# Another order for the minima and low parts of the neighbourhood attention, and stick-breaking weights stored column by column

## The chip, the core and the metric

The kernel runs on one core of one Trainium2 chip. The metric is the device time of one execution in microseconds (us); three runs of the kernel before gave 1026.44 to 1029.01, median 1027.77. One further execution was recorded by the profiler, and every row below comes from it.

The engines by the names of the profile: PE is TensorE (matmuls), PEld its weight loads, DVE VectorE, ACT ScalarE, POOL GpSimd, SP the queue that issues most loads.

## What is computed

The kernel is a chain of two networks in fp32 over 256 tokens of width 1024: two layers (a pooling mixer, then stick-breaking attention, each followed by a gated feed-forward), then a third layer with neighbourhood attention and a long convolution side by side, a gated merge and a feed-forward. The change touches two places.

Stick-breaking attention (16 heads of 64, 272 tokens, the first 16 of them meta tokens that are keys for all):

```python
z = jnp.einsum('bqhd,bkhd->bhqk', q, k) * (HEAD_DIM ** -0.5)
mask = kpos[None, :] < qpos[:, None]
log_keep = jnp.where(mask, jax.nn.log_sigmoid(-z), 0.0)
later = lax.cumsum(log_keep, axis=3, reverse=True) - log_keep
a = jnp.where(mask, jnp.exp(jax.nn.log_sigmoid(z) + later), 0.0)
return jnp.einsum('bhqk,bkhd->bqhd', a, v)
```

Neighbourhood attention (8 heads of 64; 256 keys of the grid, rotated, with a bias, and 256 context keys):

```python
s_nb = jnp.einsum('brqhd,brikhd->bhrqik', grid(q_rot), k_band) * scale + bias[None]
s_nb = jnp.where(col_ok[:, None, :], s_nb, NEG_INF)
s_ctx = jnp.einsum('brqhd,bchd->bhrqc', grid(q), k_ctx) * scale
p = jax.nn.softmax(jnp.concatenate([s_nb, s_ctx], axis=-1), axis=-1)
o = p_nb @ v_band + p_ctx @ v_ctx
```

Beside it a short convolution over 12 column blocks of 128 (`hy`), whose first eight results are turned for a long convolution.

## The kernel before

**Products.** Each fp32 operand is split into a high part (fp32r, ScalarE's copy) and a low part (the difference, VectorE), and a product is three matmuls: high x high, low x high, high x low. Weights arrive as `raw` (three buffers of 1 MB, loaded by SP as soon as the low parts made from the old contents exist), are cast by ScalarE into `wh` and lowered by VectorE into `wl`. Such a piece of 128x1024 is a "half"; six halves are held, and a half may be written once the half six places earlier is spent. `casts` (line 430) and `rests` (line 447) issue every cast or low part that has become possible up to a given point; `rests` can be limited by `most`.

**The order.** Each engine runs a written queue in order; waits are on semaphores that count named moments. So the order of the calls in `sb_pe`, `sb_act`, `sb_dve` (stick-breaking) and `second_pe`, `second_act`, `second_dve`, `second_pool` (neighbourhood) is the order of the work.

**Stick-breaking, lines 1291 to 1716.** The loop runs over p = 0 to 7, pairs of heads (h = 0, 1), and in each over two query tiles (qt = 0: 152 keys, qt = 1: 272 keys). Per pair TensorE makes the scores (`scores_pe`), the projections of q and k for pair p+2 and of v for pair p+1, turns v (`vt_pe`) and the weights (`turns_pe`), and sums the output of pair p-1 (`out_pe`). Keys 32 to 151 and 152 to 271 are turned in two pieces of 120. The first 32 keys are the tail: both heads' tails lie above each other in 64 rows, so that `out_pe` handles both in one group of three matmuls. Before, head 0's tail is turned by a transpose into rows 0 to 31, and head 1's into rows 32 to 63 by `turn` (line 1312), an ordinary fp32 product with the identity matrix; the row shows it as a MATMUL of line 93, a transpose as one of line 96. ScalarE makes |z|, exp, ln (`softs`), the final exponential `weights` into `as_[2h+qt]`, and the high parts `ath`, `tth`; VectorE makes the maximum (`soft`), the scan (`later`), the difference (`kept`) and the low parts `atl`, `ttl`, `vl`; `kvf` scales a projection out of PSUM.

**Neighbourhood, lines 1917 to 2336.** The loop runs over p = 0 to 3, each with two heads (h) and two query tiles (qt), kk = 4p + 2h + qt. Per step kk: `na_scores` on TensorE (12 or 6 matmuls into bank 3 or 4), `least` on VectorE (adds the bias of buffer kk % 3, takes the minimum of the negative), `soft` on ScalarE (exponential with its sum), `shares` on VectorE (reciprocal, scaling), `na_turn` (four transposes), `ath`/`atl` for the high and low parts, `na_av`, then `oh`/`ol`. The queries are rotated: `perm_pe`, `turn1`, `turn2`, then high and low parts `quh`, `qul`, `qrh`, `qrl` into `QQ`, whose other head's 64 rows must be zero. POOL adds the bias and the mask (`b`, kk) into BB. The convolution blocks are `hy_pe`, `conv` on both engines, `hy_turn` and `turned`.

Of the kernel before, what the change touches and what calls it, by code (L numbers as in the profile page):

```python
# [238 lines left out]
class Kernel:  # L239
# [252 lines left out]
    def memory_sb(self):  # L492
# [17 lines left out]
        self.as_ = [at(f"a{i}", T1) for i in range(4)]  # L510
# [822 lines left out]
    def turns_pe(self, P, p, h, qt):  # L1333
        S, a = self.S, self.as_[2 * h + qt]
        if qt == 0:
            self.claim(P, 5 + h, (S["sb_v"], ("atl", p, h)))
        if h + qt == 0:
            self.claim(P, 7, (S["sb_v"], ("ol", p)))
        tb, o_bank = self.ps[5 + h], self.ps[7]
        P.wait_ge(S["sb_a"], ("at", p, h, qt))  # L1340
        if qt == 0:
            P.tr(tb[0:120, 256:384], a[:, 32:152], self.ident)
            self.turn(P, o_bank, h, slice(0, 128), a[:, 0:32]).then_inc(S["sb_p"], ("t", p, h, 0))
        else:
# [4 lines left out]
    def out_pe(self, P, p):
# [101 lines left out]
    def sb_act(self, A):  # L1451
# [1628 lines left out]
```

## Time and profile before

| | |
|---|---|
| timed runs | 1026.44, 1027.77, 1029.01 us, median 1027.77 |
| profiled execution | 1023.1 us, its span 1020.8 us |
| TensorE / its weight loads | 984.4 us (96%) / 952.7 us (93%) of the span |
| VectorE | 823.2 us (81%) |
| ScalarE | 565.0 us (55%) |
| GpSimd | 110.7 us (11%) |
| HBM traffic | 192.17 MB, 188 GB/s on average |

Busy time is an average over stages. Stick-breaking runs from about 255 to 387 us of the span and the neighbourhood stage from about 621 to 712 us; each has to be read by itself. A matmul's end is modelled in these rows, so that TensorE shows itself busy for some tenths of a microsecond in which nothing new is issued; the start of the next weight load is the better mark. TensorE's granted clock is full throughout both stages.

### The profile page before, as it was taken

How to read it: one execution, taken by the hardware profiler on the slowest of the kernel's cores; microseconds unless marked ns; L12 is line 12 of the kernel's file. 1: busy time of each engine (PE TensorE's matmuls, PEld its weight loads, DVE VectorE, ACT ScalarE, POOL GpSimd, SP SyncE). 2: the span in 40 equal slices, each digit the busy share in tenths (PEclk: the TensorE clock that was granted, in tenths of full speed). 3: DMA queues.
4: the chain of work that ended last, by engine and by line, in shares of the span. 5: the costliest groups of instructions: out<-in, count | busy, mean ns of one | idle time of the engine just before them, and what ended most of it. 6: DMA issues, size and time to landing. Idle time of an engine off the chain costs nothing.

```text
span 1020.8 us, 19465 instructions
## 1 busy us (share of the span) xinstructions
PE 984.4 (96%) x7932; PEld 952.7 (93%) x7932; DVE 823.2 (81%) x1386; ACT 565.0 (55%) x1062; POOL 110.7 (11%) x128
## 2 busy tenths in 40 slices
PE   7999999999999999999999999899999999999996
PEld 6899999999888889999999998888999989999996
DVE  7989898887889867999979868888998668776543
ACT  6745454445766646555554535665554466665432
POOL 4100000111000004002203310221001100000000
PEclk9999999999999999999999999999999999999999
DMA  9554657665433314888867813333335436555441
GB/s 283 229 194 184 239 204 243 238 238 195 147 134 101 128 62 172 341 317 301 288 222 287 312 39 148 139 107 113 134 138 210 162 124 218 212 190 175 159 164 41
DMA packets 33880, 192.17 MB, mean 188 GB/s; under 512 B 4976, under 2 KB 6272, under 8 KB 15104
## 3 DMA queue, kind: packets, MB, share of 16 engines
q1 hardware_dynamic: 23440, 157.36, 42.7%
q10 hardware_dynamic: 6912, 25.17, 7.3%
q0 software_dynamic: 3440, 8.42, 2.7%
q8 instruction: 62, 1.02, 0.4%
q14 instruction: 26, 0.21, 0.1%
HBM read 187.78 MB, written 3.15 MB: 187 GB/s over the span
## 4 chain that ended last, share of the span: by engine, by line
PE 70%; DVE 19%; ACT 6%; issue 3%; DMA 1%; POOL 0%; DVEq 0%; ACTq 0%; POOLq 0%
PE ps L93 69%; DVE wl L70 6%; ACT wh L67 2%; DVE a L70 1%; DVE b L70 1%; DVE natl L70 1%; PE ps L96 1%; DMA raw<-w 1%; ACT s L67 1%; DVE s L84 1%; DMA fz<-fz 1%; DVE s L77 1%; DVE x L73 0%; DVE tmp L73 0%; DVE x L70 0%
## 5 line engine op out<-in xcount | busy, mean ns | idle before, releaser
L70 DVE TENSOR_TENSOR wl<-raw,wh 128x1024 fp32r<-128x1024 f32 x283 | 342.6, 1225 | 22.7 <-ACT wh L67 22.3
L67 ACT ACTIVATE wh<-raw 128x1024 fp32r<-128x1024 f32 x286 | 296.2, 1049 | 25.1 <-PE ps L93 10.2
L93 PE MATMUL ps<-xh,wh 128*128 128x256 f32 (+1 forms) x992 | 278.4, 281 | 4.2 <-DVE wl L70 2.7
L93 PE MATMUL ps<-xh,wl 128*128 128x256 f32 (+1 forms) x992 | 276.8, 279 | 0.0
L93 PE MATMUL ps<-xl,wh 128*128 128x256 f32 x992 | 275.7, 278 | 0.0
L93 PE MATMUL ps<-xt,wh 128*128 128x272 f32 (+1 forms) x1120 | 218.3, 290 | 2.2 <-DVE fg L70 1.0
L93 PEld LDWEIGHTS ps<-xh,wh 128*128 128x128 f32 x992 | 186.7, 188 | 5.5 <-issue 2.4
L93 PEld LDWEIGHTS ps<-xl,wh 128*128 128x128 f32 x992 | 187.1, 189 | 0.0
L93 PEld LDWEIGHTS ps<-xh,wl 128*128 128x128 f32 x992 | 186.7, 188 | 0.2
L93 PEld LDWEIGHTS ps<-xt,wh 128*128 128x128 f32 x1120 | 177.4, 188 | 5.4 <-issue 2.0
L93 PE MATMUL ps<-xt,wl 128*128 128x272 f32 (+1 forms) x560 | 160.1, 286 | 0.0
L93 PE MATMUL ps<-hl,wh 128*128 128x256 f32 (+1 forms) x528 | 149.7, 283 | 0.0
L93 PE MATMUL ps<-hh,wh 128*128 128x256 f32 (+1 forms) x528 | 149.6, 283 | 0.0
L93 PE MATMUL ps<-hh,wl 128*128 128x256 f32 (+1 forms) x528 | 149.6, 283 | 0.0
L93 PEld LDWEIGHTS ps<-xt,wl 128*128 128x128 f32 x560 | 105.7, 189 | 0.3
L93 PEld LDWEIGHTS ps<-hl,wh 128*128 128x128 f32 x528 | 100.5, 190 | 0.0
L93 PEld LDWEIGHTS ps<-hh,wh 128*128 128x128 f32 x528 | 99.4, 188 | 0.1
L93 PEld LDWEIGHTS ps<-hh,wl 128*128 128x128 f32 x528 | 99.1, 188 | 0.0
L67 ACT ACTIVATE hh<-fh 128x256 fp32r<-128x256 f32 (+1 forms) x66 | 27.9, 422 | 102.9 <-DVE fh L70 79.1
L70 POOL TENSOR_TENSOR acc<-acc,sq 128x256 f32<-128x256 f32 (+1 forms) x30 | 33.7, 1124 | 443.0 <-ACT sq L67 443.0
L67 ACT ACTIVATE sq<-x 128x256 f32<-128x256 f32 (+1 forms) x43 | 17.6, 420 | 96.7 <-DVE x L70 51.4
L84 DVE CUSTOM_DVE_ANT_0 ada<-ada,cb 128x1024 f32<-128x1024 f32 x42 | 57.2, 1361 | 0.1
(350 smaller groups left out, 1596.8 us busy)
## 6 DMA issues: line engine op xcount, KB each, us to landing
raw<-w SPq DMA_DIRECT2D x141, 1024.0 KB, 4.9
ada<-ada ACTq DMA_DIRECT2D x42, 512.0 KB, 4.5
cb<-ada ACTq DMA_DIRECT2D x6, 512.0 KB, 4.2
raw<-w SPq DMA_DIRECT2D x4, 512.0 KB, 6.5
spare<-w SPq DMA_DIRECT2D x2, 1024.0 KB, 9.6
spectra<-ev POOLq DMA_DIRECT2D x8, 256.0 KB, 4.9
skew<-rpb POOLq DMA_DIRECT2D x8, 192.0 KB, 3.6
x<-x POOLq DMA_DIRECT2D x2, 544.0 KB, 9.1
```

Source lines behind the costliest of these rows:

```text
L67: return Issued(self.e and self.e.activation(out, src, func, **kw))
L70: return Issued(self.e and self.e.tensor_tensor(out, a, b, op))
L77: return Issued(self.e and self.e.tensor_scalar(out, src, s1, s2, op0=op0))
L84: return Issued(self.e and self.e.tensor_tensor_reduce(out, a, b, scale, start, op0, op1, accum))
L93: return Issued(self.e and self.e.matmul(out, stat, mov, start=start, stop=stop))
L96: return Issued(self.e and self.e.transpose(out, src, ident))
```

## The change

In stick-breaking attention the four weight tiles `as_` become one tile `aw`, in which the two heads of one query tile lie column by column (head 0 in the even columns, head 1 in the odd ones). The first 64 columns hold the first 32 keys of both heads, so that one transpose of 64 columns turns both tails; it is issued with head 1's turns, and the tail's rows are now interleaved. The same is done for v: `vf` is written without its first 32 keys, which go into a 64-column tile `vtail` in two steps of 64 rows with stride-two writes (the other head's columns are zero), and one transpose turns it. The copies and low parts of the v tail become one 64x128 step each. `turn` is gone.

In the neighbourhood stage the eight zero fills of `QQ` go from VectorE (64 rows each) to GpSimd (128 rows each), where they stand ahead of the bias sums; for p < 3, `least(4p+3)` and `shares(4p+3)` go from the start of the next pair to the end of their own, around `atl`; the DFT table's split (FH, FL) goes from before the loop to behind `conv(0)`; some low parts of the first pair are issued later; and TensorE makes the first two scores of p = 0 before `hy_pe(2)`, as for the others.

The diff, cut to its core:

```diff
-        self.as_ = [at(f"a{i}", T1) for i in range(4)]
+        self.aw = at("a", 4 * T1)
+        self.vtail = [area(f"vt{i}", 64) for i in range(2)]
...
-        P.tr(b[0:32, 256:384], f[:, 0:32], self.ident)
-        self.turn(P, b, 1, slice(256, 384), f[:, 0:32]).then_inc(S["sb_p"], ("vt", p))
-
-    def turn(self, P, bank, h, c, a):
-        if h == 0:
-            return P.tr(bank[0:32, c], a, self.ident)
-        return P.mm(bank[32:64, c], a, self.ident, True, True)
+        P.tr(b[0:64, 256:384], self.vtail[p % 2][:, :], self.ident).then_inc(S["sb_p"], ("vt", p))
+
+    def weight(self, h, qt):
+
+        return self.aw[:, 2 * T1 * qt + h:2 * T1 * (qt + 1):2]
...
+        S, a = self.S, self.weight(h, qt)
         if qt == 0:
             self.claim(P, 5 + h, (S["sb_v"], ("atl", p, h)))
-        if h + qt == 0:
+        if h and qt == 0:
             self.claim(P, 7, (S["sb_v"], ("ol", p)))
         tb, o_bank = self.ps[5 + h], self.ps[7]
         P.wait_ge(S["sb_a"], ("at", p, h, qt))
         if qt == 0:
-            P.tr(tb[0:120, 256:384], a[:, 32:152], self.ident)
-            self.turn(P, o_bank, h, slice(0, 128), a[:, 0:32]).then_inc(S["sb_p"], ("t", p, h, 0))
+            o = P.tr(tb[0:120, 256:384], a[:, 32:152], self.ident)
         else:
             P.tr(tb[0:120, 384:512], a[:, 32:152], self.ident)
-            P.tr(tb[0:120, 128:256], a[:, 152:272], self.ident)
-            self.turn(P, o_bank, h, slice(128, 256), a[:, 0:32]).then_inc(S["sb_p"], ("t", p, h, 1))
+            o = P.tr(tb[0:120, 128:256], a[:, 152:272], self.ident)
+        if h:
+            o = P.tr(o_bank[0:64, 128 * qt:128 * (qt + 1)], self.aw[:, 2 * T1 * qt:2 * T1 * qt + 64], self.ident)
+        o.then_inc(S["sb_p"], ("t", p, h, qt))
...
-            for k in (0, 1):
-                s = slice(32 * k, 32 * k + 32)
-                A.act(th[s, 64 * k:64 * k + 64], b[s, 256 + 64 * k:320 + 64 * k], ACT.Copy).then_inc(
-                    S["sb_a"], ("wth", p, k))
+            A.act(th[:, :], b[0:64, 256:384], ACT.Copy).then_inc(S["sb_a"], ("wth", p))
...
-            A.act(self.as_[i][:, :w], self.cs[(4 * p + i) % 3][:, :w], ACT.Exp).then_inc(S["sb_a"], ("at", p, h, qt))
+            A.act(self.weight(h, qt)[:, :w], self.cs[(4 * p + i) % 3][:, :w], ACT.Exp).then_inc(S["sb_a"], ("at", p, h, qt))
...
+        def vf(p):
+
+            f, ft, b = self.vf[p % 2], self.vtail[p % 2], self.ps[self.bank[("v", p)]]
+            if p > 1:
+                V.wait_ge(S["sb_p"], ("vt", p - 2))
+            V.wait_ge(S["sb_g"], ("zero",))
+            V.wait_ge(S["proj"], ("v", p))
+            V.tt(f[:, 32:], b[:, 32:T1], R[:, 32:], ALU.mult).then_inc(S["sb_v"], ("vmain", p))
+            for k in (0, 1):
+                s = slice(64 * k, 64 * k + 64)
+                o = V.tt(ft[s, k:64:2], b[s, 0:32], R[s, 0:32], ALU.mult)
+            o.then_inc(S["sb_v"], ("vf", p))
...
-            for k in (0, 1):
-                s, c = slice(32 * k, 32 * k + 32), slice(64 * k, 64 * k + 64)
-                V.tt(tl[s, c], b[s, 256 + 64 * k:320 + 64 * k], th[s, c].bitcast(F32), ALU.subtract).then_inc(
-                    S["sb_v"], ("wtl", p, k))
+            V.tt(tl[:, :], b[0:64, 256:384], th[:, :].bitcast(F32), ALU.subtract).then_inc(S["sb_v"], ("wtl", p))
...
-            if p:
-                self.na_scores(P, p, 0, 0), self.na_scores(P, p, 0, 1)
+            self.na_scores(P, p, 0, 0), self.na_scores(P, p, 0, 1)
             self.hy_pe(P, 3 * p + 2)
-            if p == 0:
-                self.na_scores(P, p, 0, 0), self.na_scores(P, p, 0, 1)
...
-        A.wait_ge(S["ld_dftf"], ("load",))
-        A.act(self.FH[:, :], self.dftf[:, :], ACT.Copy).then_inc(S["hy_a"], ("tab", 0))
         for p in range(4):
             qf(p), quh(p, 0), quh(p, 1)
             self.casts(A, W.spent(("nq", p)))
...
                     turned(3 * p - 1)
                 ath(2 * p - 1, 0), ath(2 * p - 1, 1)
             conv(3 * p)
+            if p == 0:
+                A.wait_ge(S["ld_dftf"], ("load",))
+                A.act(self.FH[:, :], self.dftf[:, :], ACT.Copy).then_inc(S["hy_a"], ("tab", 0))
...
-        V.wait_ge(S["na_p"], ("v", 3))
-        for i, s in enumerate(self.QQ):
-            for t in s:
-                r0 = 64 * (1 - i)
-                o = V.memset(t[r0:r0 + 64, :].bitcast(F32), 0.0)
-        o.then_inc(S["na_v"], ("zero",))
         vl(2), vl(3), vl(0), vl(1)
-        self.rests(V, first + 8)
-        V.wait_ge(S["hy_a"], ("tab", 0))
-        V.tt(self.FL[:, :], self.dftf[:, :], self.FH[:, :].bitcast(F32), ALU.subtract).then_inc(S["hy_v"], ("tab", 0))
+        self.rests(V, first + 8, most=3)
         for p in range(4):
-            if p:
-                least(4 * p - 1), shares(4 * p - 1)
             qul(p, 0), qul(p, 1)
             turn1("q", p)
             if p:
                 ol(2 * p - 2)
-            self.rests(V, W.spent(("nq", p)))
+            if p > 1:
+                self.rests(V, W.spent(("nq", p)))
             if p:
                 atl(2 * p - 1, 0), atl(2 * p - 1, 1)
             conv(3 * p)
-            turn2("q", p), qrl(p, 0), qrl(p, 1)
-            self.rests(V, W.spent(("hy", 3 * p)))
+            if p == 0:
+                V.wait_ge(S["hy_a"], ("tab", 0))
+                V.tt(self.FL[:, :], self.dftf[:, :], self.FH[:, :].bitcast(F32), ALU.subtract).then_inc(
+                    S["hy_v"], ("tab", 0))
+            turn2("q", p)
+            if p == 0:
+                qrl(p, 0), qrl(p, 1)
+                self.rests(V, W.spent(("nq", 0)))
+            else:
+                qrl(p, 0), qrl(p, 1)
+                self.rests(V, W.spent(("hy", 3 * p)))
             if p:
                 ol(2 * p - 1)
             conv(3 * p + 1)
-            self.rests(V, W.spent(("hy", 3 * p + 1)))
+            if p:
+                self.rests(V, W.spent(("hy", 3 * p + 1)))
             least(4 * p), least(4 * p + 1), shares(4 * p), shares(4 * p + 1)
+            if p == 0:
+                self.rests(V, W.spent(("hy", 0)))
             conv(3 * p + 2)
             least(4 * p + 2)
-            self.rests(V, W.spent(("hy", 3 * p + 2)))
+            if p:
+                self.rests(V, W.spent(("hy", 3 * p + 2)))
+            if p < 3:
+                least(4 * p + 3)
             atl(2 * p, 0), atl(2 * p, 1), shares(4 * p + 2)
+            if p < 3:
+                shares(4 * p + 3)
+            if p == 0:
+                self.rests(V, W.spent(("hy", 2)))
...
+        G.wait_ge(S["na_p"], ("v", 3))
+        for s in self.QQ:
+            for t in s:
+                o = G.memset(t[:, :].bitcast(F32), 0.0)
+        o.then_inc(S["na_g"], ("zero q",))
```

## Rows read from the trace of the kernel before

**Rows 1.** The page, section 4: the chain that ended last, shares by engine.
```profile
PE 70%; DVE 19%; ACT 6%; issue 3%; DMA 1%; POOL 0%; DVEq 0%; ACTq 0%; POOLq 0%
```

**Rows 2.** Busy us (instructions) of PE, PEld, DVE, ACT, POOL; clock, DMA, GB/s.
```profile
282.50:298.35 15.85, 15.85 (x121) 14.05 (x120) 14.03 (x31) 10.81 (x29) 0.00 (x0) 1.00 0.20 67
...
650.31:672.11 21.80, 20.27 (x168) 19.39 (x168) 18.95 (x39) 13.86 (x30) 4.99 (x6) 1.00 0.32 115
```

**Rows 3.** PEld in stick-breaking, timeline: start, us, operation, count [idle <-releaser].
```profile
279.25 0.54 PEld L96 LDWEIGHTS ps<-cst,a 128*120 128x120 f32 x5
...
270.90 0.27 PEld L96 LDWEIGHTS ps<-cst,vf 128*120 128x120 f32 x3
...
271.37 0.14 PEld L93 LDWEIGHTS ps<-cst,vf 128*32 128x32 f32 x2 [0.21 <-issue]
...
271.71 0.19 PEld L93 LDWEIGHTS ps<-kh,qh 128*128 128x128 f32 x1 [0.20 <-issue]
...
281.94 0.14 PEld L96 LDWEIGHTS ps<-cst,a 128*120 128x120 f32 x1 [0.21 <-ACT a L67]
...
282.53 0.19 PEld L93 LDWEIGHTS ps<-xt,wh 128*128 128x128 f32 x1 [0.20 <-issue]
```

**Rows 4.** PEld by form, 624 to 716: count | busy, mean ns | idle.
```profile
L96 PEld LDWEIGHTS ps<-cst,s 128*128 128x128 f32 x64 | 7.0, 140 | 8.1 <-DVE s L77 7.8
...
L96 PEld LDWEIGHTS ps<-cst,tmp 128*128 128x128 f32 x16 | 2.5, 206 | 1.8 <-DVE tmp L73 1.8
```

**Rows 5.** Timelines of ACT and DVE in one stick-breaking pair.
```profile
286.39 0.49 ACT L67 ACTIVATE ath<-ps 120x384 fp32r<-120x384 f32 x1 [2.03 <-PE ps L93]
...
286.92 0.56 DVE L70 TENSOR_TENSOR atl<-ps,ath 120x384 fp32r<-120x384 f32 x1 [0.56 <-ACT ath L67]
...
289.51 0.76 DVE L73 SCALAR_TENSOR_TENSOR l<-ps,l 128x152 f32<-128x152 f32 x2 [0.58 <-ACT l L67]
...
297.40 0.33 ACT L67 ACTIVATE a<-c 128x152 f32<-128x152 f32 x1 [0.68 <-DVE c L70]
```

**Rows 6.** Groups by form, DVE, whole run: a small step out of PSUM.
```profile
L70 DVE TENSOR_TENSOR wtl<-ps,wth 32x64 fp32r<-32x64 f32 x16 | 3.3, 209 | 0.3
```

**Rows 7.** Timelines of DVE and PE, neighbourhood pair p = 1 and its end.
```profile
661.69 0.68 DVE L84 CUSTOM_DVE_ANT_0 s<-ps,bias 128x512 f32<-128x512 f32 x1
...
668.02 1.29 DVE L70 TENSOR_TENSOR natl<-ps,nath 128x512 fp32r<-128x512 f32 x2 [0.23 <-ACT nath L67]
...
671.39 0.16 DVE L87 RECIPROCAL small<-small 128x1 f32<-128x1 f32 x1 [0.88 <-ACT s L67]
...
672.13 0.66 PE L96 MATMUL ps<-cst,s 128*128 128x128 f32 x4 [1.01 <-DVE s L77]
```

**Rows 8.** Timelines of DVE, ACT and PE, first neighbourhood pair.
```profile
621.50 0.27 DVE L90 MEMSET nqh<- 64x256 f32 x1 [3.13 <-PE ps L93]
...
624.16 0.60 ACT L67 ACTIVATE vvh<-ps 128x512 fp32r<-128x512 f32 x1 [0.78 <-PE ps L93]
...
634.60 0.50 PE L96 MATMUL ps<-cst,tmp 128*128 128x128 f32 x2 [1.61 <-DVE tmp L73]
...
639.91 0.69 DVE L84 CUSTOM_DVE_ANT_0 s<-ps,bias 128x512 f32<-128x512 f32 x1
```

**Rows 9.** Timelines of POOL and DVE: zero fills of BB, bias sums, low part.
```profile
598.52 0.83 POOL L90 MEMSET bias<- 128x256 f32 x3
...
599.30 1.44 POOL L70 TENSOR_TENSOR bias<-skew,cmask 128x256 f32<-128x256 f32 x2
...
644.94 1.66 POOL L70 TENSOR_TENSOR bias<-skew,cmask 128x256 f32<-128x256 f32 x1 [1.89 <-DVE small L84]
...
644.77 1.23 DVE L70 TENSOR_TENSOR wl<-raw,wh 128x1024 fp32r<-128x1024 f32 x1
```

**Rows 10.** Timeline of PE behind the stage; the page's section 6, weight loads.
```profile
738.03 0.38 PE L93 MATMUL ps<-yh,gh 128*128 128x256 f32 x1 [0.57 <-DVE yl L70]
...
raw<-w SPq DMA_DIRECT2D x141, 1024.0 KB, 4.9
```

More of the change, by code:

```diff
@@ L1304, in vt_pe @@
         S, f = self.S, self.vf[p % 2]
-        b = self.next_bank(P, ("vt", p), (S["sb_v"], ("wtl", p, 1)))
+        b = self.next_bank(P, ("vt", p), (S["sb_v"], ("wtl", p)))
         P.wait_ge(S["sb_v"], ("vf", p))
@@ L1353, in out_pe @@
         P.wait_ge(S["sb_v"], ("vl", p))
-        P.wait_ge(S["sb_v"], ("wtl", p, 1))
+        P.wait_ge(S["sb_v"], ("wtl", p))
         P.wait_ge(S["sb_v"], ("ttl", p))
@@ L1444, in sb_pool @@
                 G.memset(self.pad(t, 1).bitcast(F32), 0.0)
-            for t in (th, tl):
-                o = G.memset(t[:, :].bitcast(F32), 0.0)
+        for t in self.vtail:
+            o = G.memset(t[:, :], 0.0)
         o.then_inc(S["sb_g"], ("zero",))
@@ L1510, in weights @@
             if p:
-                A.wait_ge(S["sb_p"], ("t", p - 1, h, qt))
+                A.wait_ge(S["sb_p"], ("t", p - 1, 1, qt))
             else:
@@ L1603, in ql, with kf @@
             V.tt(l[s, c], self.qf[p % 2][s, :], h[s, c].bitcast(F32), ALU.subtract).then_inc(S["sb_v"], ("ql", p, k))
-        def kvf(k, p):
-            f = (self.kf if k == "k" else self.vf)[p % 2]
+        def kf(p):
             if p > 1:
-                V.wait_ge(*((S["sb_v"], ("kl", p - 2)) if k == "k" else (S["sb_p"], ("vt", p - 2))))
+                V.wait_ge(S["sb_v"], ("kl", p - 2))
             V.wait_ge(S["norm_v"], ("r", "m1"))
-            V.wait_ge(S["proj"], (k, p))
-            V.tt(f[:, :], self.ps[self.bank[(k, p)]][:, :T1], R[:, :], ALU.mult).then_inc(S["sb_v"], (k + "f", p))
+            V.wait_ge(S["proj"], ("k", p))
+            V.tt(self.kf[p % 2][:, :], self.ps[self.bank[("k", p)]][:, :T1], R[:, :], ALU.mult).then_inc(
+                S["sb_v"], ("kf", p))
+        def vf(p):
[9 more added lines that the diff above has]
+            o.then_inc(S["sb_v"], ("vf", p))
         def kl(p):
@@ L1621, in vl @@
             b = self.ps[self.bank[("vt", p)]]
[L1622 removed]
+            V.wait_ge(S["sb_a"], ("wth", p))
             V.tt(self.pad(l), b[0:120, 0:256].rearrange("p (t k c) -> p t k c", t=2, k=2), self.pad(h).bitcast(F32),
                  ALU.subtract).then_inc(S["sb_v"], ("vl", p))
[L1625 to L1628 removed]
+            V.tt(tl[:, :], b[0:64, 256:384], th[:, :].bitcast(F32), ALU.subtract).then_inc(S["sb_v"], ("wtl", p))
         def part(p, h, qt):
@@ L1670, in sb_dve @@
         for p in (0, 1):
-            qf(p), kvf("k", p), ql(p, 0), ql(p, 1), kl(p)
+            qf(p), kf(p), ql(p, 0), ql(p, 1), kl(p)
             self.rests(V, W.spent(("k", p)))
-        kvf("v", 0)
+        vf(0)
         for p in range(8):
@@ L1695, in sb_dve @@
                 ql(p + 2, 1)
-                kvf("k", p + 2)
+                kf(p + 2)
                 self.rests(V, W.spent(("k", p + 2)), True)
@@ L1701, in sb_dve @@
             if p < 7:
-                kvf("v", p + 1)
+                vf(p + 1)
             atl(p, 1)
@@ L1939, in na_scores @@
         P.wait_ge(S["na_v"], ("krl", p))
-        P.wait_ge(S["na_v"], ("zero",))
+        P.wait_ge(S["na_g"], ("zero q",))
         P.wait_ge(S["na_v"], ("qul", p, h))
@@ L2067, in quh @@
                 A.wait_ge(S["na_p"], ("s", 4 * p - 3 + 2 * h))
-            A.wait_ge(S["na_v"], ("zero",))
+            A.wait_ge(S["na_g"], ("zero q",))
             A.wait_ge(S["na_a"], ("qf", p))
@@ L2252, in least @@
                 V.wait_ge(S["na_p"], ("t", kk - 3))
-            V.wait_ge(S["na_v"], ("zero",))
+            V.wait_ge(S["na_g"], ("zero q",))
             V.wait_ge(S["na_g"], ("b", kk))
```

2 lines of the change are left out of this document (removed).

## The prediction

> **What bounds the kernel now.** I read the chain that ended last first, then the busy time by stretch, then each engine's timeline in the two stages that the diff touches. Over the whole run TensorE carries 70% of the chain [rows 1], so the question is whether the two stages are among the exceptions. They differ. In the stick-breaking stage (255 to 387 us) one pair of heads takes 15.85 us, TensorE has no idle time in it and VectorE is busy 14.03 us; in the neighbourhood stage (621 to 712 us) one pair takes 21.80 us, VectorE is busy 18.95 us, and its weight-load column shows TensorE free for some 2.4 us of it [rows 2]. So stick-breaking is set by TensorE with the softmax loop close behind, and the neighbourhood stage by VectorE's queue with the waits inside it.
>
> **Stick-breaking, TensorE.** Three transposes hold the weight load for 0.27 us, five for 0.54 [rows 3]; I take 0.09 us each and 0.1 for the way back to ordinary work. Head 1's part of the 32-key tail is no transpose but a true fp32 product against the identity: two passes with an idle weight load of 0.20 us before and after. The block of vt_pe (three transposes and one such product) takes 0.81 us; with three transposes alone 3 x 0.09 + 0.1 = 0.37, so 0.44 is saved. The block of turns_pe(1,0) takes 0.59; two transposes take 0.28, so 0.31 is saved [rows 3]. turns_pe(1,1) has one transpose more and should save between the two, 0.39. Head 0's block loses two of its five transposes: 0.18. Sum 1.32 us per pair. The six long transposes now load every second column. The nearest rows: a stride-two load of tmp is busy 0.206 us, a packed one 0.140 [rows 4]; six times 0.066 would be 0.4. Packed loads are issued well under 0.140 apart (three in 0.27), so most of such a time overlaps, and I take 0.1. TensorE's own time per pair falls by 1.2 to 14.65 us.
>
> **Stick-breaking, the loop behind it.** That much is not to be had, since turns_pe(1,0) already waits 0.21 us for ScalarE's weights [rows 3]. The loop: turns_pe(1,0) at 281.94, the value projection, turns_pe(1,1), ScalarE's ath at 286.39, then tth, a cast, abs, exp, ln, VectorE's first maximum at 289.51 (after 0.58 idle), VectorE without a gap to the difference that feeds the exponential at 297.40, and turns_pe(1,0) again, 15.85 after its last start [rows 5]. What it loses: 0.31 in turns_pe(1,0); about 0.23 in turns_pe(1,1) up to its last result (the way back isn't on this path), less 0.02 for strides; and on VectorE one of two tail subtractions. Those are 32x64 at 0.21 us each [rows 6]; one 64x128 in their place I take at 0.3, 0.18 less with the gap between them. Sum 0.52 + 0.18 = 0.70. The new vf makes one product into three: the long one is 32 columns shorter, and each small one has 64x32 elements, half the row length of the 32x64 ones (0.21 [rows 6]), so up to 0.4 more. It stands ahead of atl(1) and ttl on VectorE's queue, where VectorE now waits 0.56 us for ath [rows 5]; that wait hides it, and without the wait it would cost 0.4 per pair. ScalarE's second tail copy (0.21) goes too, off the loop. ScalarE's exponentials now write every second word. No row of the kernel before shows such a write on ScalarE; from the packed 0.33 us I take no change, and as the far end a doubling, +0.33 on the loop. VectorE's queue time is 15.85 - 1.54 of named idle = 14.3, plus 0.2 net, 14.5: it isn't the bound. So the pair goes to 15.15 us: 0.7 x 5 = 3.5 us for the five steady pairs (turns_pe(1,0) from 266.08 to 345.36).
>
> The ends: pair 0 gains 0.2 (the tail copy stands ahead of its exponentials; vf's extra 0.4 is taken up by a later wait of VectorE for ScalarE). From 345.36 to the end of pair 6 the projections and the output matmuls fill TensorE, and its savings count in full: 0.31 + 0.39 + 0.44 + 0.18 + 0.31 + 0.23 = 1.86, less 0.1 for strides; pair 7's chain runs over ScalarE's tail copies, another 0.15. After turns_pe(7,1,0), which waits for ScalarE, 0.31 + 0.39 remain. Stage: 0.2 + 3.5 + 1.9 + 0.7 = **6.3 us**. The feed-forward layer behind it fills TensorE, so the gain is kept.
>
> **Neighbourhood, steady pairs.** VectorE idles in five places: 0.27, 0.23 (atl waits for ath), 0.88 (shares(4p+3) waits for its exponential, right behind least(4p+3)), 0.46 (ol) and 0.48 (qrl) (two of them in [rows 7]). With least(4p+3) ahead of atl and shares(4p+3) behind shares(4p+2), the exponential runs beside atl: ath has 0.65 us more, the 0.23 and the 0.88 go, and ol comes behind an output matmul that is no longer stalled, for 0.4 more. TensorE's wait of 1.01 us for shares(4p+3) [rows 7] goes with it. least(4p+3) needs scores(1,1), done 1.2 us before VectorE reaches it; if they were late, atl, shares(4p+2) and TensorE's na_av would queue behind it. The pair goes from 21.80 to about 20.4; TensorE's floor is 21.8 - 2.1 of stalls = 19.7. Two pairs (p = 1 and 2) give 2.8 us; pair 3 keeps its order.
>
> **Neighbourhood, the first pair.** Eight zero fills leave VectorE (0.27 each, behind 3.13 us of waiting for the v projection [rows 8]). But vl's last step waits for ScalarE's copy of the last v bank at 624.16, so only 0.66 us is gained there. Walking on with the same durations: vl ends at 625.45, three low parts at 629.2, qul to 630.3, conv(0) at 631.35 (0.6 idle, for ScalarE), the table's low part, the turn, qrl to 635.05, two low parts, conv(1), least(0) at 638.25 against 639.91 [rows 8]. TensorE loses its 1.61 us wait at hy_turn [rows 8] and finds about 1.5 us at the scores moved ahead of hy_pe(2), since qrl(0,0) is ready at 634.65. Then the deferred low parts come due: six between least(0) and least(4) where there were four, 2 x 1.14 = 2.3 us, less 1.1 of waits saved, so that least(4) comes at 661.3 against 661.69 [rows 7]. The first pair yields **0.4 us**. The loads behind deferred halves stay ahead: SP's load behind half 181 is issued at 642.8, lands some 4.9 us later [rows 10] and is cast after 651. The POOL fills: 128x256 took 0.28 us each [rows 9], eight 2.2 us from 621.4, done at 623.7, where ScalarE first needs them at 629.4. On POOL's queue the bias sums stand behind them; three at 0.75 are ready at 626, needed at 638. Stage: 0.4 + 2.8 = **3.2 us**, kept, since VectorE also sets the pace of the following stage (TensorE waits for it at 738 [rows 10]) and nothing there is tied to an outer event.
>
> The bias sums now run at 624 to 626 us, beside vl and VectorE's first low part. In the trace a low part that had started 0.2 us before a bias sum took 1.23 us, as any other, and the bias sum 1.66 instead of 0.72 [rows 9]: POOL, the later one, gave way. The Trainium skill (SBUF — State Buffer, section "SBUF: two separate sides") has it that a VectorE operation with two SBUF inputs and a GpSimd operation that reads SBUF exclude each other for a whole instruction, and that whoever starts first wins; by that rule the first low part may be held back by the rest of the third bias sum, up to 0.72 us, and the stage would give 2.5 us instead of 3.2. The row agrees with the rule for the case where VectorE is first; no row shows POOL first.
>
> **The sum.** 6.3 + 3.2 = 9.5 us. The profiled execution took 1023.1 us around a span of 1020.8; it becomes 1013.6. It lies 4.7 us under the median of the timed runs, 1027.77, with the same kernel; against the median the sum gives **1018.3 us** (0.991).
>
> **Rivals.** (a) The loop doesn't bind and TensorE's full 1.2 us per pair comes off: 0.5 x 5 more, 1015.8. Against it: the 0.21 us wait that stands there already. 12%. (b) VectorE binds: vf's small steps cost like whole ones (0.4 each), or the exponentials double; then 0.3 to 0.4 of the 0.7 goes, the stage gives 4, the time is 1020.5. For it: VectorE at 14.5 of 15.15. 18%. (c) The neighbourhood order only moves the waits: the first pair's new stalls grow, or low parts are held back by POOL, and 0.5 to 1 us is left: 1020.8. For it: my own walk, where 1.66 us gained at least(0) shrank to 0.4. 12%. (d) Both (b) and (c), and less: within 3 us of before. 7%. (e) Slower: ScalarE's stride-two writes. Its exponentials take 1.52 us of 10.8 busy per pair; if a strided write took k times as long, ScalarE would bind from k = 4.5 on; at k = 6 the pair is 18.2 us, seven pairs cost 16.5, and the time is 1027.8 + 16.5 - 3.2 = 1041. Against it: TensorE's strided load is busy only half as long again. 3%, and 1% for the sum of small things. (f) The forecast, 1016.3 to 1020.3: 47%.
>
> **How the numbers follow.** (a) to (c) and (f) are 89% and faster by more than 0.3%, about the least that a measurement of this kernel can tell from no change; (d) is no change, (e) slower: 0.89, 0.07, 0.04. The range takes in (a) with the profiled run's offset, so down to 1012.5, and (b) and (c) to 1023.
>
> **What would show it.** Right: turns_pe(1,0) starts 15.1 to 15.2 us apart with a wait of 0.4 to 0.7 us for ScalarE; no fp32 product in the turns; 0.88 gone from shares(4p+3), pairs 20.4 us apart, least(0) 1.7 us earlier but least(4) only 0.4 us (each after taking off the first stage's shift). Wrong: a pair of 15.6 (VectorE or ScalarE binds) or 14.7 (no loop); a low part behind a bias sum at 626; a long ScalarE exponential.

## The result and the profile after

Four runs of the changed kernel took 1009.55 to 1012.26 us, median **1011.57 us**; with a fourth run beside it the kernel before has the median 1027.11. The ratio is 0.9859, 95% interval 0.9838 to 0.9880: faster, and by more than the forecast's 9.5 us (0.991). A second set of runs, on other occasions (r1 below), gave 1010.38 against 1020.13 us, 0.9897 [0.9875, 0.9919]; one run of the kernel before in that set took 1202.17 us at a granted clock of 0.753, and the ratio leaves it out. The changed kernel repeats; the kernel before was 7 us slower in the first set. So the gain is between 9.8 and 15.5 us, and the traces must say what of it is the change.

The profiled executions: span 1007.5 us against 1020.8, 13.3 less. Where one and the same operation stands in both traces, after less before:

| point | shift, us |
|---|---|
| TensorE, first scores of stick-breaking | +0.18 |
| first addition of the stage's output to x (382.84 before) | -7.03 |
| end of the second feed-forward layer | -7.91 |
| first rotation of k, ahead of the neighbourhood stage | -8.94 |
| least(12) | -12.25 |
| TensorE, first product with gh (738.03 before) | -12.24 |
| third feed-forward layer, middle / end | -10.94 / -13.25 |

Stick-breaking gave 7.21 us (forecast 6.3), the neighbourhood stage 3.31 (forecast 3.2). The other 2.74 came where the diff changes nothing.

Busy time by stretch of the changed kernel, columns as in [rows 2], one pair of each stage:

```profile
280.97:295.92 14.95, 14.53 (x114) 13.74 (x115) 14.05 (x32) 10.42 (x29) 0.00 (x0) 1.00 0.23 82
652.30:672.87 20.57, 19.22 (x161) 18.42 (x160) 18.80 (x41) 14.02 (x29) 5.01 (x6) 1.00 0.35 120
```

The pairs are 14.95 and 20.57 us long where they were 15.85 and 21.80. VectorE's busy time in the stick-breaking pair did not fall (14.05 us where it was 14.03): the stage is fuller, not emptier.

The weight loads of that stick-breaking pair (to be held against [rows 3]):

```profile
280.97 0.22 PEld L96 LDWEIGHTS ps<-cst,a 128*120 128x120 f32 x2 [0.49 <-DVE c L70]
...
284.19 0.34 PEld L96 LDWEIGHTS ps<-cst,a 128*120 128x120 f32 x3
...
285.34 0.19 PEld L96 LDWEIGHTS ps<-cst,vf 128*120 128x120 f32 x2 [0.25 <-DVE vt L70]
285.50 0.11 PEld L96 LDWEIGHTS ps<-cst,vt 128*64 128x64 f32 x1
...
295.92 0.22 PEld L96 LDWEIGHTS ps<-cst,a 128*120 128x120 f32 x2 [0.50 <-DVE c L70]
```

No load of line 93 is left among them: the true fp32 products and their 0.20 us on either side are gone. Two things are new. turns_pe(1,0) waits 0.50 us, which the forecast had said (0.4 to 0.7). And vt_pe waits 0.25 us for vf's small products, which it had not. The releaser named in the first and last row is VectorE's c, but c is only what ScalarE's exponential reads; what turns_pe(1,0) needs is that exponential's result `a`, which ends at 295.80 (295.46 and 0.34 long, below), just ahead of the load at 295.92.

ScalarE and VectorE in the same pair (to be held against [rows 5] and [rows 6]):

```profile
284.84 0.49 ACT L67 ACTIVATE ath<-ps 120x384 fp32r<-120x384 f32 x1 [1.50 <-PE ps L96]
286.43 0.56 ACT L67 ACTIVATE u<-ps 128x152 f32<-128x152 f32 x2
...
291.17 0.38 ACT L67 ACTIVATE oh<-ps 128x256 fp32r<-128x256 f32 x1 [0.58 <-PE ps L93]
...
295.46 0.34 ACT L67 ACTIVATE a<-c 128x152 f32<-128x152 f32 x1 [0.69 <-DVE c L70]
```

```profile
284.90 0.38 DVE L70 TENSOR_TENSOR vt<-ps,r 64x32 f32<-64x32 f32 x2
285.36 0.56 DVE L70 TENSOR_TENSOR atl<-ps,ath 120x384 fp32r<-120x384 f32 x1
...
287.79 0.76 DVE L73 SCALAR_TENSOR_TENSOR l<-ps,l 128x152 f32<-128x152 f32 x2 [0.42 <-ACT l L67]
...
290.35 0.27 DVE L70 TENSOR_TENSOR wtl<-ps,wth 64x128 fp32r<-64x128 f32 x1
290.55 0.40 DVE L73 SCALAR_TENSOR_TENSOR qf<-ps,r 128x256 f32<-128x256 f32 x1
...
294.05 0.32 DVE L73 SCALAR_TENSOR_TENSOR l<-ps,l 128x152 f32<-128x152 f32 x1 [0.15 <-ACT l L67]
```

And the one step of the kernel before that the forecast had passed over, ScalarE's abs of head 0:

```profile
287.99 0.73 ACT L67 ACTIVATE u<-ps 128x152 f32<-128x152 f32 x2
```

The exponential writes every second word in 0.34 us (0.33 before). atl(1) follows vf without a wait where it waited 0.56. The two abs take 0.56 where they took 0.73. The one tail subtraction, 0.27 us long, frees VectorE 0.20 us after its start (290.35 to 290.55).

The neighbourhood stage, first VectorE, then GpSimd, then TensorE (to be held against [rows 7] and [rows 8]):

```profile
616.79 1.90 DVE L70 TENSOR_TENSOR wl<-raw,wh 128x1024 fp32r<-128x1024 f32 x1 [0.25 <-ACT wh L67]
618.62 1.21 DVE L70 TENSOR_TENSOR wl<-raw,wh 128x1024 fp32r<-128x1024 f32 x1
...
622.39 1.00 DVE L73 SCALAR_TENSOR_TENSOR tmp<-ps,cst,tmp 128x255 f32<-128x255 f32 x2 [0.18 <-ACT tmp L67]
...
629.36 0.68 DVE L84 CUSTOM_DVE_ANT_0 s<-ps,bias 128x512 f32<-128x512 f32 x1
...
638.61 0.15 DVE L87 RECIPROCAL small<-small 128x1 f32<-128x1 f32 x1
...
652.30 0.68 DVE L84 CUSTOM_DVE_ANT_0 s<-ps,bias 128x512 f32<-128x512 f32 x1
...
672.87 0.68 DVE L84 CUSTOM_DVE_ANT_0 s<-ps,bias 128x512 f32<-128x512 f32 x1
```

```profile
614.27 0.31 POOL L90 MEMSET nqrl<- 128x256 f32 x1
...
616.86 0.75 POOL L70 TENSOR_TENSOR bias<-skew,cmask 128x256 f32<-128x256 f32 x1
```

```profile
625.84 0.36 PE L93 MATMUL ps<-kkh,nqrh 128*128 128x256 f32 x1 [1.69 <-DVE nqrl L70]
```

The wait of 0.88 us ahead of shares(4p+3) is gone (638.61 has none). TensorE waits 1.69 us at the moved scores (forecast 1.5). A low part of 1.90 us, where the next takes 1.21, stands beside the third bias sum (616.86).

### The profile page after: what moved, and what is told of

It reads as the page before. It is cut to its first block, busy times and chain, and to the rows that moved or that the text cites. A ratio compares the mean times of both kernels' runs of the same rounds, so it can differ in the third digit from the quotient of the medians.

```text
span 1007.5 us, 19368 instructions
## 1 busy us (share of the span) xinstructions
PE 970.8 (96%) x7884; PEld 947.9 (94%) x7884; DVE 821.9 (82%) x1386; ACT 563.0 (56%) x1054; POOL 111.5 (11%) x134
## 4 chain that ended last, share of the span: by engine, by line
PE 67%; DVE 19%; ACT 8%; issue 3%; DMA 2%; POOL 0%; SPq 0%; DVEq 0%; ACTq 0%
PE ps L93 66%; DVE wl L70 6%; ACT wh L67 3%; DMA raw<-w 2%; PE ps L96 1%; DVE a L70 1%; DVE b L70 1%; ACT u L67 1%; DMA cst<-cst 1%; DVE s L77 1%; DVE c L81 1%; DVE l L73 1%; ACT s L67 1%; DVE natl L70 0%; ACT a L67 0%
```

## The experiments

All were profiled; a ratio is against the kernel before, run on the same occasion. The kernels e3, e4, k3, n1, n2, n3 and s1 have one timed run each, the profiled one, so they are read by their traces alone. Read from each trace: the stick-breaking stage (first scores to first addition to x), its pair (mean of the five from pair 0 to pair 5), then from the first rotation of k to least(0) and to least(4), the pairs p = 1 and 2, and a tile of the third feed-forward layer's second half.

| kernel | stage | pair | least(0) | least(4) | p = 1, 2 | tile |
|---|---|---|---|---|---|---|
| before | 127.08 | 15.86 | 36.31 | 58.09 | 21.80, 21.80 | 7.77 |
| after | 119.87 | 14.93 | 34.70 | 57.64 | 20.57, 20.17 | 7.48 |
| e1_sb_only | 119.93 | 14.93 | 36.30 | 58.09 | 21.79, 21.79 | 7.77 |
| e2_na_only | 127.15 | 15.86 | 34.72 | 57.66 | 20.47, 20.28 | 7.77 |
| e3_turns_only | 121.96 | 15.18 | 36.30 | 58.09 | 21.80, 21.79 | 7.77 |
| e4_tail_only | 123.43 | 15.33 | 36.33 | 58.12 | 21.79, 21.79 | 7.77 |
| s1_tail_twice | 121.33 | 15.11 | 34.72 | 57.65 | 20.49, 20.27 | 7.77 |
| k1_vt_later | 118.52 | 14.69 | 34.71 | 57.64 | 20.47, 20.18 | 7.77 |
| k3_vt_later_cast_later | 118.55 | 14.69 | 34.70 | 57.64 | 20.46, 20.27 | 7.48 |
| k4_all_three | 117.44 | 14.47 | 34.70 | 57.63 | 20.46, 20.29 | 7.48 |
| n1_least_late | 119.93 | 14.92 | 34.71 | 62.52 | 21.78, 21.78 | 7.77 |
| n2_fills_vector | 119.95 | 14.92 | 34.70 | 57.63 | 20.46, 20.19 | 7.48 |
| n3_scores_late | 119.80 | 14.91 | 34.70 | 57.63 | 20.46, 20.18 | 7.48 |
| r1_changed_again | 119.82 | 14.92 | 34.71 | 57.65 | 20.56, 20.18 | 7.48 |

**The two parts apart.** e1 has the diff's hunks up to `sb_dve`, e2 those from `na_scores` on.

> The whole stick-breaking part of the change alone, the neighbourhood stage as before. Between the two traces (before, changed) the stick-breaking stage gave 7.2 us and the neighbourhood stage 3.3; the other 2.8 us of 13.3 came in stages that the diff doesn't touch (the second and third feed-forward layers). If the parts are independent: turns_pe(1,0) 14.95 us apart, the stage ends 7.2 us earlier, the neighbourhood pairs keep their 21.80, and the whole is 7 to 10 us faster (0.990 to 0.993). If the gain outside the stages hangs on the change as a whole (another place of the instructions or tiles) it is anything between 5 and 10 us; if it hangs on the stick-breaking part, near 10.

> The neighbourhood part alone (fills to GpSimd, low parts deferred, scores and minima moved), stick-breaking as before. Mine: pairs 20.6 and 20.2 us apart where they were 21.80, the stage gives 3.3 us, 0.9968 of the time before. Rival: part of the 3.3 us came from a better phase after the shorter stick-breaking stage (loads in time), then 2 us or less. With what the untouched stages vary by, the whole lies between 2 and 6 us faster.

e1: 0.9921 [0.9900, 0.9942]; e2: 0.9972 [0.9953, 0.9990]. The product is 0.9893, the forecast's 0.991 and r1's 0.9897 within its error. Each stage moves as it does in the whole, to 0.1 us (table), so the parts are independent. Both have the slow tile of 7.77 us.

**Stick-breaking in halves.** In both, the 32-key rows of weights and of v are in different orders (one side interleaved, the other not), so the tails' product is not the reference's; the instructions are the same.

e3 has `weights` and `turns_pe` as changed, and vf, vt_pe, wth and wtl as before:

```diff
+        self.aw = at("a", 4 * T1)
...
         self.turn(P, b, 1, slice(256, 384), f[:, 0:32]).then_inc(S["sb_p"], ("vt", p))
```

e4 the other way round:

```diff
         self.as_ = [at(f"a{i}", T1) for i in range(4)]
+        self.vtail = [area(f"vt{i}", 64) for i in range(2)]
...
+        P.tr(b[0:64, 256:384], self.vtail[p % 2][:, :], self.ident).then_inc(S["sb_p"], ("vt", p))
```

> Of the stick-breaking part only the interleaved weights and the joint transposes in turns_pe; vf, vt_pe and the tail of v as before, the neighbourhood as before. By my forecast's steps the loop loses 0.31 in turns_pe(1,0) and 0.21 in turns_pe(1,1): pair 15.33 us. By the rival reading of the changed trace (a term of the loop was missed in the tail part, because vt_pe stands between the two scores of head 0 that ScalarE waits for) the same 15.3 here, and the missing 0.2 us is in e4. If instead the turns save more on the path than I reckoned: 15.1. Slower than 15.85 if strided writes of ScalarE cost.

> Of the stick-breaking part only the 32-key tail of v: vf in three products, one joint transpose in vt_pe, one copy and one subtraction; the weights and turns_pe as before. By my forecast's steps only one tail subtraction is on the loop: 15.85 - 0.18 = 15.67 us a pair, and the 0.44 us saved in vt_pe is off it. By the rival reading vt_pe's saving brings scores(0,1) forward, for which ScalarE's second abs waits, and this part alone gives 0.35 to 0.45: 15.4 to 15.5 us. If VectorE bound, vf's 0.4 would show and the pair be 15.8 or more.

Measured 0.67 and 0.53 us less a pair, together 1.20, where the whole gives 0.93. Expected were 0.52 and, by the forecast, 0.18; the rival reading had 0.35 to 0.45 for e4, so both parts gave more than either account. Three rows of each, ScalarE's abs, VectorE's step behind the tail subtractions and head 1's first maximum; e3, with turns_pe(1,0) at 281.57:

```profile
287.01 0.59 ACT L67 ACTIVATE u<-ps 128x152 f32<-128x152 f32 x2
...
291.44 0.42 DVE L73 SCALAR_TENSOR_TENSOR qf<-ps,r 128x256 f32<-128x256 f32 x1
...
294.89 0.32 DVE L73 SCALAR_TENSOR_TENSOR l<-ps,l 128x152 f32<-128x152 f32 x1
```

and e4, with turns_pe(1,0) at 281.06:

```profile
287.11 0.56 ACT L67 ACTIVATE u<-ps 128x152 f32<-128x152 f32 x2
...
291.23 0.41 DVE L73 SCALAR_TENSOR_TENSOR qf<-ps,r 128x256 f32<-128x256 f32 x1
...
294.60 0.32 DVE L73 SCALAR_TENSOR_TENSOR l<-ps,l 128x152 f32<-128x152 f32 x1
```

The second abs needs scores(p,0,1), and vt_pe stands ahead of those on TensorE. Before, the two abs took 0.73 us, in e3 0.59 and in e4 0.56: either half brings the scores forward, so 0.14 to 0.17 us belongs to both and is counted twice in their sum. That is the term that the forecast missed when it left the saving in vt_pe, and turns_pe(1,1)'s way back to ordinary work, out of the loop. Most of the rest of the difference stands at head 1's first maximum: it starts 3.45 us behind the step after the tail in e3 and 3.37 in e4 (3.44 before), but 3.50 in the changed kernel, where it waits for ScalarE. (e3's one run took 1016.44 us, e4's 1018.43.)

**How much slack VectorE has.**

```diff
                 s = slice(64 * k, 64 * k + 64)
+                V.tt(self.vmore[s, k:64:2], b[s, 0:32], R[s, 0:32], ALU.mult)
                 o = V.tt(ft[s, k:64:2], b[s, 0:32], R[s, 0:32], ALU.mult)
```

> The changed kernel, with vf's two small products (64x32, 0.19 us each) made twice, the second time into a tile that nobody reads: 0.38 us more of VectorE per pair in front of atl(1) and ttl. My theory, that the loop through TensorE and ScalarE binds and VectorE has slack (it waits 0.42 us for the first ln of the next pair): pair 14.95 to 15.05 us. Rival, VectorE's queue is what binds at 14.95 and where the gain above my 15.15 ended: pair 15.3 us.

15.11: neither. Both numbers had priced the added products at 0.38 us, and they took 0.20. From the first small product to atl(1) it is 0.62 us instead of 0.46, and the last small product ends 0.59 us behind the first's start instead of 0.38:

```profile
285.49 0.17 DVE L70 TENSOR_TENSOR vm<-ps,r 64x32 f32<-64x32 f32 x1
...
286.11 0.56 DVE L70 TENSOR_TENSOR atl<-ps,ath 120x384 fp32r<-120x384 f32 x1
```

TensorE's wait at vt_pe grew by the same 0.20, and ScalarE's wait ahead of oh with it:

```profile
286.13 0.19 PEld L96 LDWEIGHTS ps<-cst,vf 128*120 128x120 f32 x2 [0.45 <-DVE vt L70]
...
291.94 0.39 ACT L67 ACTIVATE oh<-ps 128x256 fp32r<-128x256 f32 x1 [0.76 <-PE ps L93]
```

From 0.25 to 0.45 us, and the pair from 14.93 to 15.11: what the products took reached the pair nearly whole. That number alone would suit a loop over VectorE's queue as well. The waits speak against that one: VectorE's for head 0's ln fell from 0.42 to 0.26, but its wait for ScalarE ahead of head 1's first maximum rose from 0.15 to 0.34. So at 14.93 the path seems to lead from vf's products through TensorE (vt_pe, the q projection, out_pe) to oh, a cast and head 1's abs; k1 below settles it.

**The loop that binds after.** Three variants of the changed kernel. All have the first of these edits, k3 and k4 the second (for p > 0), k4 alone the third (for p < 6):

```diff
-            if 0 < p < 7:
-                self.vt_pe(P, p)
             self.scores_pe(P, p, 0, 1)
+            if 0 < p < 7:
+                self.vt_pe(P, p)
...
-                self.casts(A, W.spent(("q", p + 2)))
                 softs(p, 1)
+                self.casts(A, W.spent(("q", p + 2)))
...
-                self.kv_pe(P, "v", p + 1)
+                self.kv_pe(P, "v", p + 1, 0, 3)
             self.turns_pe(P, p, 1, 1)
+                self.kv_pe(P, "v", p + 1, 3)
```

> The changed kernel with vt_pe behind scores(p,0,1) instead of between head 0's two scores. My theory of the 14.95 us: two loops lie within 0.15 us of each other, one through VectorE's queue behind ath(1), one through TensorE (turns_pe(1,0), the v projection, scores(0,0), a wait of 0.25 us for vf's small products ahead of vt_pe, q projection, out_pe) to ScalarE's oh, a cast and head 1's abs. The wait goes, so TensorE's loop loses 0.25 and the pair falls by no more than VectorE's queue lets it, 0.1 us: 14.85. Rival: TensorE's loop alone binds, pair 14.70. Other rival: TensorE isn't on it, pair 14.95.

> As k1_vt_later, and ScalarE's cast of the weights' half that stands between its q copy and head 1's abs (0.95 us) comes behind head 1's ln. The loop over oh gets up to 0.4 us of slack more, until head 1's scores are what abs waits for. If VectorE's queue binds after k1, nothing changes: 14.85; if the loop over oh binds, 14.5. Slower (15.2 or more) if the later cast holds up VectorE's low part or TensorE's products of that half.

> As k3_vt_later_cast_later, and the v projection is cut behind its third tile, with turns_pe(1,1) in the gap. ath(1) needs turns_pe(1,1), which in the changed kernel waits behind the whole projection though its weights are ready 1.8 us earlier (ScalarE is idle 1.50 us ahead of ath). This takes the projection out of the loop over ath: its start comes 1.5 us earlier, head 0's abs then waits for its scores, VectorE's first maximum comes 0.4 us earlier, and the pair goes to 14.4 to 14.6 us, near TensorE's own 14.2 to 14.3. Rival: TensorE's extra break costs as much as it gives (0.1 per break), or VectorE's vf, now ahead of a ready atl(1), becomes the bound: 14.8 or more.

k1: 14.69, 0.24 us less and so practically the whole wait of 0.25; my 14.85 was too careful about VectorE's queue. ScalarE's oh now waits 0.23 us for TensorE, and VectorE has no wait left ahead of head 1's maxima. k3: nothing, 14.69 (one run, 1007.76 us), so after k1 the loop over oh isn't what binds. k4: 14.47, as expected; ath(1) starts 2.15 us behind turns_pe(1,0) (282.75 against 280.60), where it started 3.87 behind (284.84 against 280.97). Rows of k1, then of k4:

```profile
291.22 0.38 ACT L67 ACTIVATE oh<-ps 128x256 fp32r<-128x256 f32 x1 [0.23 <-PE ps L93]
...
296.08 0.22 PEld L96 LDWEIGHTS ps<-cst,a 128*120 128x120 f32 x2 [0.61 <-DVE c L70]
```

```profile
282.75 0.48 ACT L67 ACTIVATE ath<-ps 120x384 fp32r<-120x384 f32 x1
...
295.05 0.22 PEld L96 LDWEIGHTS ps<-cst,a 128*120 128x120 f32 x2 [0.21 <-issue]
```

k4's stick-breaking stage is 2.4 us shorter than the changed kernel's, which no other stage gives back. Its time was 1008.51 us against 1021.69, 0.9865 [0.9845, 0.9886], k1's 1009.42, 0.9866 [0.9842, 0.9890]. That beats the kernel before; that it beats the changed one is shown in the stage alone, since the two were not timed beside each other and the ratios overlap.

**The neighbourhood change, piece by piece undone.**

n1 takes back the move of least(4p+3), n2 that of the fills, n3 that of the first pair's scores:

```diff
         for p in range(4):
+            if p:
+                least(4 * p - 1), shares(4 * p - 1)
...
-            if p < 3:
-                least(4 * p + 3)
             atl(2 * p, 0), atl(2 * p, 1), shares(4 * p + 2)
-            if p < 3:
-                shares(4 * p + 3)
```

```diff
-                o = G.memset(t[:, :].bitcast(F32), 0.0)
...
+                o = V.memset(t[r0:r0 + 64, :].bitcast(F32), 0.0)
```

```diff
+            if p:
+                self.na_scores(P, p, 0, 0), self.na_scores(P, p, 0, 1)
             self.hy_pe(P, 3 * p + 2)
+            if p == 0:
+                self.na_scores(P, p, 0, 0), self.na_scores(P, p, 0, 1)
```

> The changed kernel, but least(4p+3) and shares(4p+3) again stand at the head of the next pair, as before; the rest of the neighbourhood change stays. Mine: the waits of 0.23 (atl) and 0.88 (shares) come back and the pairs go from 20.57 and 20.17 back to 21.6 or more; least(0) stays where it is (629.36 less what the stages ahead differ by), and least(4) comes 0 to 0.5 us later. Rival: the deferred low parts and the scores bring the pairs down, and this move alone gives less than half: pairs of 21.0 or less.

The pairs are back at 21.78, so the move of least(4p+3) is worth all 1.2 and 1.6 us of them. But least(4) came 4.9 us later, where 0 to 0.5 was expected. VectorE, TensorE and again VectorE of n1:

```profile
643.37 0.68 DVE L84 CUSTOM_DVE_ANT_0 s<-ps,bias 128x512 f32<-128x512 f32 x1
...
651.58 0.48 DVE L73 SCALAR_TENSOR_TENSOR tmp<-ps,cst,tmp 128x255 f32<-128x255 f32 x1 [2.10 <-ACT tmp L67]
```

```profile
645.68 0.66 PE L96 MATMUL ps<-cst,s 128*128 128x128 f32 x4 [3.56 <-DVE s L77]
```

With the low parts deferred, two of them stand ahead of a late least(3); shares(3) comes at 645.14, TensorE waits 3.56 us for it with hy_pe's next products behind, and the convolution at 651.58 waits 2.10 us for what follows from those. Part of that is TensorE's clock. Busy 0.94 of the 4.5 us from 642.0 to 646.5, it then had a granted clock of 0.5 (1.2 GHz) for 3.41 us from 647.04, just when those products ran; columns of the first row as in [rows 2]:

```profile
647.00:650.40 3.40, 3.40 (x19) 3.40 (x18) 1.71 (x3) 1.64 (x5) 0.00 (x0) 0.51 0.20 84
```

```profile
648.04 0.41 PE L93 MATMUL ps<-xh,wl 128*128 128x256 f32 x1
648.26 0.41 PE L93 MATMUL ps<-xl,wh 128*128 128x256 f32 x1
```

Sixteen products started 0.213 us apart where 0.117 is usual, an estimated 1.5 us of the 4.9. Up to least(4) n1 takes 4.4 us more than the kernel before, in one execution: some 3 of them by the waits and the rest, by that estimate, by the clock. The rest of the new order is a loss in that pair unless least(4p+3) moves too. Whether the clock falls in every execution of n1 isn't shown. (n1's one run: 1021.98 us, n2's 1011.41, n3's 1009.56, s1's 1013.93, the kernel before beside them 1022.83.)

> The changed kernel with the eight zero fills back on VectorE behind the last v projection. By my forecast they were worth 0.66 us of least(0)'s 1.66 us (the fills take 2.2 us, but vl's last step waits for ScalarE in any case), so least(0) comes 0.6 to 0.7 us later than in the changed kernel (and the three deferred low parts give the rest), least(4) and the pairs after it 0.2 to 0.7 later, not more. Rival: the fills were worth 1.3 us or more.

> The changed kernel with the first pair's scores of head 0 again behind hy_pe(2). TensorE's wait of 1.69 us for the moved scores goes; the products of hy_pe(2), 2.8 us, stand ahead of the scores instead. Mine: VectorE reaches least(0) 3.5 us after the low part of the rotated q, so the scores in the new place come at about 629.9 instead of 627.2 and least(0) waits for them some 0.5 to 1 us, least(4) 0 to 0.5 later; no gain anywhere, since VectorE sets the pace. Rival: the 1.69 us of TensorE were on the path, and least(4) comes up to 1 us earlier, which would be a better kernel.

Both changed nothing: 34.70 and 57.63 as in the changed kernel. n2, VectorE:

```profile
619.21 1.20 DVE L70 TENSOR_TENSOR wl<-raw,wh 128x1024 fp32r<-128x1024 f32 x1
...
624.51 1.00 DVE L73 SCALAR_TENSOR_TENSOR tmp<-ps,cst,tmp 128x255 f32<-128x255 f32 x2 [0.58 <-ACT tmp L67]
```

With the fills on VectorE the low parts start 0.3 us later against the rotation of k (22.43 against 22.13), but none is held up, and the convolution waits 0.58 us for ScalarE, where after waits 0.18 (622.39); it starts 27.73 us behind the rotation in both. ScalarE sets that point, and the fills' move was worth nothing in this order. For n3, TensorE reached the scores at 627.10 and not at 629.9, in time for least(0): the expected wait of 0.5 to 1 us didn't come, and the move of the scores was worth nothing either. By exclusion least(0)'s 1.6 us came from the deferred low parts and the table's place; that was not undone by itself.

**The same kernel again.**

> The changed kernel itself, a second profile of it and more times. The two stages that the diff touches gave 7.2 and 3.3 us of the 13.3 by which the first pair of traces differ; 2.8 us came in stages it doesn't touch, 1.1 of it behind 726 us, where the third feed-forward layer's second half runs 7.48 us a tile instead of 7.77 and its first half 5.78 instead of 5.72 a group. In kernels so far 7.48 and 7.77 both occur, with and without the change. If the pace belongs to the program, this profile shows 7.48 again and the time is 0.986 of before; if it belongs to the execution, 7.77 may show and the times of this kernel spread over 3 us or more. The stick-breaking pair is 14.95 and the neighbourhood pairs 20.57 and 20.17 in either case.

Six runs, 1009.44 to 1014.36 us. The tile was 7.48 us again, as expected of a pace that belongs to the program, but the ratio was 0.9897 and not the 0.986 expected with it. The profiled execution, the longest, lost 4.75 us between 487 and 521 us (groups of 5.65 instead of 4.95 us), in the second feed-forward layer, and kept both stages to 0.06 us.

## Why the prediction came out as it did

**Right.** TensorE set stick-breaking's pace with the softmax loop close behind, so not all of its saving was to be had. The saving itself was larger than the 1.2 us forecast: a pair less TensorE's waits is 15.85 - 0.21 = 15.64 before and 14.95 - 0.50 - 0.25 = 14.20 after, 1.44 less. The strided exponential costs nothing that matters (rivals (b)'s doubling and (e) fall). The ends: 7.21 less five pairs at 0.93 leaves 2.6, forecast 2.8. The neighbourhood stage: pairs 20.57 and 20.17 (20.4), first pair 0.45 (0.4), sum 3.3 (3.2), the new wait 1.69 (1.5).

**Mis-sized: the loop, 0.70 forecast, 0.90 in the pair read above.** The terms, as start times behind turns_pe(1,0), before and after: ath(1) 4.45 to 3.87, 0.58 (forecast 0.52); the two abs 0.17 shorter (forecast none); tail subtraction to next step 0.48 to 0.20, 0.28 (forecast 0.18). That is 1.03. Head 1's first maximum, now waiting for ScalarE, gives back 0.06, and from the exponential's start to turns_pe it is 0.46 us instead of 0.38, 0.08: 0.89, the pair's 0.90 but for rounding. The step that failed is the list of what the loop loses, in which vt_pe's 0.44 has no place and the way back of turns_pe(1,1) is said not to be on the path. I had followed VectorE back from its maximum to ath and had not asked what the abs in between waits for.

**Wrong place: vf's small products.** The forecast hid their 0.4 us in VectorE's wait for ath. By VectorE's own queue that held, but TensorE reads vf in vt_pe, and that wait, 0.25 us, was what bound the pair at last (s1, k1). That 0.70 came as near to 0.90 as it did is in part luck: without the wait the pair would have gained 1.16 (k1, 15.86 to 14.69), and the 0.24 that the wait took hid more than half of what the forecast had missed or taken too small.

**Right sum, wrong reason: the fills.** The 0.66 us were eaten by the wait for ScalarE at conv(0), which stood in my own walk as 0.6 idle (n2).

**The low part behind a bias sum** did come: the first took 1.90 us instead of 1.21, in each of the nine traces with the fills on GpSimd, 1.90 to 1.92 us, and not with the fills on VectorE (n2). The listed start of the bias sum is 0.07 us behind the low part's, so by the listed starts VectorE was first, and yet it was VectorE that gave 0.69 us. The forecast had allowed up to 0.72 us by the rule of the Trainium skill (SBUF — State Buffer, section "SBUF: two separate sides") that the two exclude each other and that the first to start wins. With the exclusion the trace agrees; with who wins, the listed starts don't, and who was first to ask they can't show. The 0.7 us it took off the forecast's sum was not taken: the wait for ScalarE absorbed it.

**Outside the two stages: 2.74 us, forecast none.** -0.2 ahead of stick-breaking, 0.9 in the second feed-forward layer, 1.0 up to the rotation of k, -1.3 and +2.3 in the two halves of the third. VectorE's additions to x in its second half, before and after:

```profile
1003.10 0.48 DVE L73 SCALAR_TENSOR_TENSOR x<-ps,mod,x 128x256 f32<-128x256 f32 x1 [2.36 <-PE ps L93]
1010.87 0.48 DVE L73 SCALAR_TENSOR_TENSOR x<-ps,mod,x 128x256 f32<-128x256 f32 x1 [7.29 <-PE ps L93]
```

```profile
990.14 0.48 DVE L73 SCALAR_TENSOR_TENSOR x<-ps,mod,x 128x256 f32<-128x256 f32 x1 [2.06 <-PE ps L93]
997.62 0.48 DVE L73 SCALAR_TENSOR_TENSOR x<-ps,mod,x 128x256 f32<-128x256 f32 x1 [7.00 <-PE ps L93]
```

A tile has 66 products: 0.118 us each against 0.113. The slower first half goes with it (last section).

**The number.** 1011.57 lies 6.7 us under the forecast: 1.0 in the two stages, 2.7 outside them, 0.3 between span and time, and 2.7 because the profiled execution of before lay further under its own median than that of after. It lies even 0.9 us under the range's lower end of 1012.5; as a ratio, 0.9859 of the 1027.77 that the forecast started from, it is 1013.3. Rival (a), 1015.8, was nearest in time, but its reason, a loop that doesn't bind, is not what the traces show. The second set of runs gave 0.990, close to the forecast's 0.991. In rival (e) the sum was a little off: from 10.8 and 1.52 us ScalarE would bind from k = 4.3 on, and k = 6 gives 18.4 us; nothing hangs on it.

## What to carry to other kernels

When a loop is costed, ask of every operation on it what it waits for, on every engine; a saving beside the loop that stands ahead of one such input is on it. A cheap operation added to one queue must be held against all readers of its result, not only against the next wait of its own engine. Where two orders are changed together, undo each alone, and look at TensorE's granted clock where a wait has grown: the rest of the order without the moved minimum lost 4.4 us in one pair, of which an estimated 1.5 was the clock.

## What the runs showed of the hardware

The same stretch of products, with the same operands and a granted clock of 1.00 (2.4 GHz) in the third layer's second half, ran at 0.118 us a product in eight of the fourteen traces and at 0.113 in six, with nothing between. The changed kernel had 0.113 twice; n1, whose instructions on TensorE are the same, had 0.118, and k1 0.118 beside k3's 0.113. So it isn't TensorE's instructions, nor the stick-breaking part, and it repeats with the program the one time that was tried; what sets it stays open. It is worth 2.3 us in that half-layer. But the same six traces need 112.57 us for the layer's first half (first to last fu) where the other eight need 111.54 to 111.58, again with nothing between, so that the layer as a whole gains about 1 us.

Eight zero fills of 128x256 took 0.31 us each on GpSimd and started 0.25 us apart, 2.1 us in all (612.50 to 614.58) against 2.3 on VectorE for half the rows (621.50 to 623.77).

The granted clock fell to 0.5 for 3.41 us in three of the fourteen executions between their first 15 and last 10 us: in n1 at 647.0 (above), in e3 at 635.9 with TensorE busy 2.25 of the 3.9 us before, and in e1 at 757.1 with 2.01 of 4.0 before. In e3 least(4) came at 58.09 all the same: VectorE, not TensorE, sets the pace there.
